# Products of probabilities and cached values: four pages per turn, one per column strip, instead of two

## What is computed

```python
idx, valid = moba_select(qh, means, nbf)          # 3 of the 8 past blocks, for each head and query
sel_k = cache_k[pages, offs, h_ix]
sel_v = cache_v[pages, offs, h_ix]
o = moba_attend(qh, q_pos, own_k, own_v, own_pos, sel_k, sel_v, sel_pos, valid)
...
p = jax.nn.softmax(jnp.concatenate([s_sel, s_own], axis=-1), axis=-1)
return jnp.einsum('bhqnk,bhqnkd->bhqd', p_sel, sel_v) + jnp.einsum('bhqk,bhkd->bhqd', p_own, own_v)
```

## Time and profile before

| what | value |
|---|---|
| median of three runs | 2834.62 us |
| the three runs | 2833.64, 2834.62, 2841.15 us |
| span of the profiled execution | 2840.7 us |
| its own time: the only one of the three that can hold that span | 2841.15 us (0.45 us around the span) |
| stage of the decode requests' values (first to last product of L775) | 292.1 to 707.7 us of the span |
| TensorE busy over the span | 2206.3 us (78%) |

### The profile page before, as it was taken

One profiled execution on the slowest core, in us unless ns is written; L12 is line 12 of the kernel. 1 busy time (PEld: TensorE's weight loads), 2 busy tenths in 40 slices (PEclk: granted clock), 3 DMA queues, 4 the chain that ended last, 5 costly groups with the idle time before them and its releaser, 6 DMA issues.

```text
span 2840.7 us, 34618 instructions
## 1 busy us (share of the span) xinstructions
PE 2206.3 (78%) x11456; PEld 1559.8 (55%) x11456; DVE 1339.1 (47%) x2375; ACT 413.2 (15%) x776; POOL 847.8 (30%) x598
## 2 busy tenths in 40 slices
PE   8996988998887997565556666579777787777797
PEld 5775555664776777555556655577222232222276
DVE  2000100110663115888889998985444444445423
ACT  2000001100530003111112121122000010000001
POOL 0000000000000003565546665674444444444300
PEclk9998999998668998777778777867999999999999
DMA  4357998975313426888879988999999999999732
GB/s 162 133 199 303 354 351 342 346 305 198 124 60 107 140 94 263 329 341 336 338 316 363 369 343 342 359 414 383 422 422 422 422 421 421 422 422 405 325 118 93
DMA packets 139401, 854.09 MB, mean 301 GB/s; under 512 B 16337, under 2 KB 17042, under 8 KB 53954
## 3 DMA queue, kind: packets, MB, share of 16 engines
q0 software_dynamic: 85248, 612.41, 53.0%
q1 hardware_dynamic: 53506, 238.47, 22.5%
q10 hardware_dynamic: 576, 2.36, 0.2%
HBM read 843.74 MB, written 9.44 MB: 300 GB/s over the span
## 4 chain that ended last, share of the span: by engine, by line
PE 41%; DMA 23%; issue 15%; DVE 15%; SPq 3%; ACT 2%; DVEq 1%; POOL 0%; POOLq 0%; ACTq 0%
PE ps L666 18%; DMA big<-in_vt,big 18%; PE ps L759 6%; PE ps L1008 5%; DVE big L1344 4%; DMA big<-in_u,big 3%; DVE big L1300 2%; PE ps L775 2%; PE ps L712 2%; DVE big L1296 1%; PE ps L987 1%; DMA subk<-in_v 1%; SPq L325 1%; DVE big L1305 1%; PE ps L981 1%
## 5 line engine op out<-in xcount | busy, mean ns | idle before, releaser
L445 POOL DMA_INDIRECT big<-in_u,big x288 | 509.8, 1770 | 585.2 <-DVE big L1339 452.2
L1008 PE MATMUL ps<-big 128*128 128x512 f32 (+1 forms) x1152 | 528.9, 604 | 173.1 <-DMA big<-in_vt,big 167.3
L1344 DVE CUSTOM_DVE_ANT_0 big<-big 128x2048 f32<-128x2048 f32 x216 | 494.9, 2291 | 35.1 <-DMA big<-in_u,big 25.5
L1433 DVE SCALAR_TENSOR_TENSOR aT<-big,aT 128x2048 f32<-128x2048 f32 x144 | 338.6, 2352 | 337.1 <-DMA big<-in_vt,big 336.1
L981 PE MATMUL ps<-ident,big 128*128 128x128 f32 x1152 | 242.2, 397 | 315.6 <-DMA big<-in_u,big 315.6
L1008 PEld LDWEIGHTS ps<-big 128*128 128x128 f32 (+1 forms) x1152 | 198.7, 181 | 502.3 <-issue 247.5
L445 POOL DMA_INDIRECT big<-in_vt,big x288 | 328.6, 1141 | 406.8 <-PE ps L1008 349.0
L981 PEld LDWEIGHTS ps<-ident,big 128*128 128x128 f32 x1152 | 217.6, 212 | 328.1 <-issue 328.1
L987 PE MATMUL ps<-aT,wring 128*128 128x128 f32 (+1 forms) x2304 | 316.4, 302 | 0.4 <-ACT wring L606 0.4
L987 PEld LDWEIGHTS ps<-aT,wring 128*128 128x128 f32 x2304 | 316.2, 223 | 0.6 <-ACT wring L606 0.6
L606 ACT ACTIVATE wring<-ps 128x512 f32<-128x512 f32 x288 | 169.2, 597 | 674.3 <-PE ps L981 673.5
(11 more groups left out here) (266 smaller groups left out, 1563.8 us busy)
## 6 DMA issues: line engine op xcount, KB each, us to landing
big<-in_kT SPq DMA_DIRECT2D x128, 512.0 KB, 6.4
wring<-in_w_in SPq DMA_DIRECT2D x48, 1024.0 KB, 5.2
big<-in_v SPq DMA_DIRECT2D x48, 512.0 KB, 6.6
wring<-in_v SPq DMA_DIRECT2D x32, 512.0 KB, 5.4
states<-in_v SPq DMA_DIRECT2D x32, 512.0 KB, 5.5
wring<-in_w_out SPq DMA_DIRECT2D x16, 1024.0 KB, 5.0
wring<-in_w_ple SPq DMA_DIRECT2D x16, 1024.0 KB, 4.9
subk<-in_v SPq DMA_DIRECT2D x16, 512.0 KB, 6.9
```

Of the source, the lines that this page charges most:

```text
L445: pool.indirect_dma_start(ring[:, k, :], None, table, bass.IndirectOffsetOnAxis(ap=now[:, slot, k:k + 1], axis=0)).then_inc(row_in[k], 16)
L1008: mm = pe.matmul(ps[0:w, b0 + c, :], diag[:, (s * len(ON_PE) + x) % 4, 0:w], ring[:, ON_PE[x], c * 512:(c + 1) * 512], start=first, stop=F ...
L1344: dve.tensor_tensor_reduce(prod, ring[:, k, :], cnat[:, t, :], 1.0, 0.0, ALU.mult, ALU.add, dots[:, k:k + 1]).then_inc(udve_free, 1)
L1433: dve.scalar_tensor_tensor(out=acc[t % 2], in0=ring[:, k, :], scalar=coef[:, bass.ds(turn_ * UNITS + k, 1)], in1=acc[t % 2], op0=ALU.mult, ...
```

## The change

`values` takes two pairs in a turn. It waits for both pairs' `v_in`, and then issues, for each half `c`, the four products of the strips `j = 0, 1, 2, 3`. `v_free` is raised after the second half's product of `j = 1` (first pair) and again after that of `j = 3` (second pair). The products, their weights and operands, the number of waits and of raises, and the places of `early` and of `gla_tile(b,2,1)` stay as they were; no other function is changed.

```diff
             def values(b, early):
                 pe.wait_ge(pT_out, 2 * b + 2)
-                for g in range(2 * NG):
+                for g in range(0, 2 * NG, 2):
                     if g == NG:
                         early(b)
                     if g == NG + 2:
                         gla_tile(b, 2, 1)
-                    pe.wait_ge(v_in[g % 4], (b * 2 + g // 4 + 1) * 32)
+                    for h in range(2):
+                        pe.wait_ge(v_in[(g + h) % 4], (b * 2 + g // 4 + 1) * 32)
                     for c in range(2):
-                        for pg in range(2):
-                            j = 2 * (g % 2) + pg
+                        for j in range(4):
                             mm = pe.matmul(ps[j * TS:(j + 1) * TS, 6 + c, :], sprobT[:, (g // 2) * P + j * TS:(g // 2) * P + (j + 1) * TS],
-                                           vring[2 * (g % 4) + pg][:, c * 512:(c + 1) * 512], start=(g < 2), stop=(g >= 2 * NG - 2 and j > 0),
-                                           tile_position=(0, j * TS))
-                    mm.then_inc(v_free, 1)
+                                           vring[2 * ((g + j // 2) % 4) + j % 2][:, c * 512:(c + 1) * 512], start=(g == 0),
+                                           stop=(g == 2 * NG - 2 and j > 0), tile_position=(0, j * TS))
+                            if c and j % 2:
+                                mm.then_inc(v_free, 1)
```

## The result

The changed kernel takes 2847.52 us (median of 20 runs, 2838.86 to 2862.91), the kernel before 2835.49 us (20 runs, 2832.12 to 2842.47): a ratio of 1.0039, 95% interval 1.0028 to 1.0051. It is slower by 12 us, or 0.39%. The time lies just inside the forecast range, but the likeliest case, "same", is not what happened: this is the slower rival, to which the prediction gave 0.12.

What follows compares the result with a forecast made beforehand. The prediction took a 55.8 us ring per request, through SP's load issues and pair 7's landing, to bound the kernel. Terms 0 + 0 + 0 + 2.2 us on the 2834.62 us median gave about 2837 us, range 2830 to 2848.

Steps and rivals of the forecast that it cites:

- same: Whole kernel: four strips already busy, later starts covered by pair 7's landing; +2.2 us, about 2837 us, chance 0.84.
- the slower rival: Restart of pairs 6 and 7 at pair 7's landing: clock falls a second time, +17 us, 2852 us, chance 0.12.
- Order of issue, pairs 0 to 3: Pairs 0 to 3: four strips already work at once, 3.46 us, so the new order gains 0.
- the faster rival: Pairs 0 to 3: issue order limits, four strips at once save 3.9 us a request, 31 us, 2803 us, chance 0.04.
- The rule on program order: TensorE: matmuls start and end strictly in program order; by it the change would save about 3.9 us a request.
- Raises of `v_free`: Buffer releases: pairs 0 and 1 unchanged, pair 4 up to 2.5 us later but covered by TensorE's order; 0.
- The joint wait in front of pair 4: Pair 4 waits for pair 5; both restart at 1.2 GHz, covered in requests 0 to 5, +2.2 us from 6 and 7.
- its cover: Requests 0 to 5: pair 7 lands 10.2 us after pair 5, the slow path between takes 8.3 us; 0.
- The joint wait in front of pair 6: Pair 6 waits for pair 7; both end where pair 7 ended, no second clock fall expected; 0 in requests 0 to 5.
- 2.4 us each: Slower rival's price per clock fall behind pair 7's landing, from request 1's fall before; six times that is 14.6 us.
- the ring: Request to request, 55.8 us: pair 0 done, loads 4 to 7 issued, pair 7 landed, TensorE's work to next pair 0.
- The sum's base: Profiled execution's own 2841.15 us, plus 2.2 gives 2843.4; the forecast itself used the median, 2834.62 us.

Runs made afterwards that it cites:

- with pair 7 landing early: Changed kernel with the four key pages of request b+2 issued behind value pairs 6 and 7: 0.9947 to the kernel before, 2822.77 us.
- the order of SP's loads and one misplaced piece of TensorE's work: Kernel before, key pages issued behind value pairs 6 and 7, heads of request b-1 moved to the idle stretch before pair 4: 0.9874, 2800.85 us.

## Why the prediction was right, and where it was wrong

The measured time lies inside the range by 0.5 us, and only because the range was stretched upwards for a rival with a chance of 0.12. The forecast itself, about 2837 us and "same", missed by 10.5 us; that the range held is luck.

**Order of issue, pairs 0 to 3: right.** Term 0, measured 3.46 us before and after, and 1.0003 for the order alone. The starts of `wring` and `states` side by side were evidence enough against the faster rival. The rule on program order that the prediction sets against them does not stand where it says: in the Trainium skill, page "TensorE: Matmul & The Clock Gate", it is in the section "The mechanism". The equal times of the two orders disagree with it as well.

**Raises of `v_free`: right.** The order and raises of before with the joint waits are as slow as the change, so the raises' place costs nothing that can be measured; SP's waits for `v_free` came to the same 69.5 us in eight times in both profiles:

```profile
SPq L325 <- PE ps L775: 69.5, 8, 24.5
```

**The joint wait in front of pair 4: right, with its cover.** It was to restart pairs 4 and 5 at 1.2 GHz, covered by pair 7's landing in requests 0 to 5, and to cost 2.2 us in requests 6 and 7. The restart is at 0.50 in every request. The wait alone measured about 4 us (1.0016), and requests 6 and 7 together +2.6 us in the table. The parts of that sum were off in opposite directions: the pairs' end was +0.3 us in each, not +0.9 and +0.1, and the projection half +1.2 and +0.9 us, not +0.6 (rows of 5.33 and 5.00 us). That the cover is what makes the wait cheap is shown by its loss: with pair 7 landing early the changed kernel was 11 us behind the kernel before, and products in front of pairs 4 and 5 alone took that away. What the prediction did not see is how common the low clock was there before the change: it names requests 1, 6 and 7, but pairs 4 and 5 ran at least in part at 0.50 in six of the eight requests, and only in 2 and 3 wholly at 1.00; the earlier trace rows is one of these two.

**The joint wait in front of pair 6: wrong.** The step that failed is "since the delayed projection fills the gap before pair 7, I expect no second fall of the clock there". It held in four of six requests of the profiled execution, where 1.6 to 2.0 us of idle time were left, and failed in two: in request 0, where the clock came back early enough for the projection half to take 4.15 us and 3.78 us stayed idle, and in request 1, after no more than 2.00 us. The mechanism stood in the prediction as the slower rival, with the right place. Its size was off: "2.4 us each", from request 1's fall before the change, which hit one pair and part of a projection half. Behind pair 7 the low clock lasts through both pairs, the own rows and the next projection half, and the two falls cost 6.0 and 5.0 us. So two falls, not the three that the prediction named, are enough for more than the 8.5 us that it took as its threshold, and with that price the rival deserved more than 0.12. That the medians lie 12.0 us apart is close to the price of two falls, but how many falls the other nineteen executions had is not known.

The Trainium skill's warning ("TensorE: Matmul & The Clock Gate", section "HAM oscillation — how this bites in real kernels") was the right one to weigh, and the trace agrees with it in request 0: 0.50 behind 3.78 us of waiting for a DMA. It does not do so in every request, as the last section shows. The prediction used it for the longer stretch, where it was covered, and set it aside for the shorter one, which was on the ring.

**The sum's base.** The prediction took 2841.15 us for the profiled execution's own time. In the runs since, an execution is mostly 1.5 us longer than its span (2850.64 and 2849.1), so it was rather about 2842.2 us, and none of the three. Only the 2843.4 us hangs on it, and not the forecast.

## What to carry to other kernels

Before merging two waits into one, ask what ran between them: a short burst between two waits for DMA is not only work done early, it also breaks an idle stretch in two, and what stands behind the longer stretch may run at half clock. Price such a fall by everything that follows on the path until the clock is back, not by the first instruction, and look first at stretches that end on the critical ring. And where an engine waits for loads, look at the queue that issues them: here the order of SP's loads and one misplaced piece of TensorE's work were worth 35 us, while the order of the products was worth nothing.

## What was not expected of the hardware

After 3.78 us of idle time in front of pair 7 the clock was at 0.50 when the work began (request 0), and after 2.00 us it fell while the pairs ran (request 1: 0.63 us for the first product, 1.14 for the last); after 1.56 to 1.95 us in requests 2 to 5 it held. Before the change it had also held behind 3.32 us. In the kernel that waits in front of pair 6 alone it held behind 3.34 to 3.62 us in four requests, and fell behind 3.68 and 4.21 us in two. And in the kernel before, the same idle time in front of pair 4 had both ends, in requests 2 and 4:

```profile
416.60 1.91 PE L775 MATMUL ps<-wring,xT 128*32 128x512 f32 x8 [3.02 <-DMA wring<-in_v]
...
530.49 2.90 PE L775 MATMUL ps<-wring,xT 128*32 128x512 f32 x8 [3.02 <-DMA wring<-in_v]
```

In request 2 the clock stayed at 1.00; in request 4 it went from 1.00 to 0.50 while pair 4 ran. So the length of the last idle stretch alone doesn't tell whether the clock falls, and the falls come in some requests and not in others. That would fit the wide spread of the changed kernel's runs, 24 us from the fastest to the slowest, where the kernel before has 10; that the number of falls makes this spread is not shown.
